# The last half's output: residual stored ahead, scaled tiles accumulated by DMA

## The chip, the cores and the metric

The kernel runs on one core of one Trainium2 chip. The metric is the device time of one execution in microseconds (us), and lower is better. Three runs of the kernel before took 1710.51, 1711.32 and 1711.40 us; the median is 1711.32. Beside them stands one profiled execution, from which all rows below are read.

## The reference

One inference step of a two-layer trunk over 576 tokens (512 of a prompt, 64 of a sample), D_MODEL = 1024, all in float32. Each layer ends like this:

```python
x = x + rmsnorm(merged @ w_o, g_post_mix)
f = jnp.square(jax.nn.relu(rmsnorm(x, g_pre_ffn) @ w1)) @ w2
x = x + rmsnorm(f, g_post_ffn)          # of the last layer, this x is the output
```

`rmsnorm(f, g)` is `f * rsqrt(mean(f * f) + EPS) * g`, the mean over the 1024 features of a token. The change touches only the last line of the last layer: for half of the tokens, the residual `x`, the normed `f` and their sum in the output tensor.

## The kernel before

**Layout.** Everything lies transposed: features on the 128 partitions in KC = 8 tiles, tokens along the free dimension in two halves of NH = 288 (`cols(0)`, `cols(1)`). `x`, `my` (here the output f of the feed-forward network) and the output `x_out` are thus 128 x 8 x 576. A row of one half of one tile is 288 floats, 1152 B.

**Engines.** TensorE does every product as three matmuls of split operands (lines 820 to 822). VectorE and ScalarE make the splits, the activations and the norms. SP's queue loads the weights in order of their use and stores the first half of the output. GpSimd's queue builds sums of weight blocks in DRAM: plain copies (lines 1128, 1129) and accumulating DMAs (`accum_op=ALU.add`, lines 1133, 1137, 1140), done by 1085 us of the span; behind that it does nothing until the tail.

**The last layer's end.** The second matrix w2 gives 16 output tiles, eight of the first half and then eight of the second (`w2_two`); VectorE adds each onto `my` (L3076). The first half's norm and residual (L2162, L2165) are made while the second half is still multiplied, and SP stores that half whole (L1107). For the second half ScalarE writes each tile of `my`, times its gain, into `last` (L2027) and squares it (L1234). When the last square is there, TensorE sums over the features (L4035), ScalarE takes the root (L2037), VectorE inverts it (L3444) and TensorE spreads the factor per token over all partitions into PSUM (L4048). The residual `x[:, :, cols(1)]` is final since the output projection of this layer and is only read from there on.

**The tail** then does, for the eight tiles of the second half, in groups given by two lists (L275), `TAIL_MOVED` = (0, 1), (1, 3), (3, 4) and `TAIL_ADDED` = (4, 6), (6, 8):

- VectorE multiplies `last` by the factor, group by group in that order (L3450), raising `tail_factored` each time;
- for the moved groups GpSimd adds `last` onto `x` (L1196) and raises `tail_moved`, upon which SP stores the group (L1110);
- for the added groups VectorE itself adds (L3453) behind its five products and raises `tail_added`, upon which ScalarE's queue stores the group (L2041).

SP's last instruction waits for all stores (`x_stored`, L1111). Nothing but these semaphores and the order of each engine's instructions, written out by hand, sets the order.

Of the kernel before, what the change touches and what calls it, by code (L numbers as in the profile page):

```python
# [9 lines left out]
ALU = mybir.AluOpType  # L10
# [7 lines left out]
DEPTH = 2  # L18
# [12 lines left out]
KC = D // P  # L31
# [22 lines left out]
def n_head(h, i):  # L54
    return N_P1 + N_HEAD * h + i
# [216 lines left out]

TAIL_MOVED, TAIL_ADDED = [(0, 1), (1, 3), (3, 4)], [(4, 6), (6, 8)]  # L275
TRI = NH // 3

G_PRE, G_POST, G_FF, G_FPOST, G_Q, G_KV, G_CONV = 0, 8, 16, 24, 32, 35, 37
# [69 lines left out]
def root(L, name):  # L348
    return len(ROOTS) * L + ROOTS.index(name) + 1
# [9 lines left out]
def x_new(L, name, m):  # L359
    return 32 * L + NEW[name] + m + 1  # L360
# [6 lines left out]
class Plan:  # L367


    def __init__(self, nc, ctx):  # L370
# [8 lines left out]
        def semaphore(name):  # L379
            return ctx.enter_context(nc.semaphore(name))  # L380
# [111 lines left out]
        self.tail_full = semaphore("tail_full")  # L492
        self.tail_factored = semaphore("tail_factored")
        self.tail_added = semaphore("tail_added")
        self.tail_moved = semaphore("tail_moved")

        self.ff_read = semaphore("ff_read")
        self.ff_inverted = semaphore("ff_inverted")
# [309 lines left out]
def cols(s):  # L808
    return slice(NH * s, NH * (s + 1))
# [40 lines left out]
def program(nc, x_in, consts, tables, blocks, small, uv, cache_t, cache_n, cache_pe,  # L850
            x_out, kv_out, kpe_out, conv_out):
    with ExitStack() as ctx:
        pl = Plan(nc, ctx)
        block = ctx.enter_context(nc.Block())
        loads(nc, block, pl, x_in, consts, tables, blocks, small, uv, cache_t, cache_n, cache_pe, x_out)
        rotation_and_sums(nc, block, pl, blocks)
        scalar_engine(nc, block, pl, x_in, x_out, kv_out, kpe_out, conv_out)
        vector_engine(nc, block, pl)
        tensor_engine(nc, block, pl)


def loads(nc, block, pl, x_in, consts, tables, blocks, small, uv, cache_t, cache_n, cache_pe, x_out):
# [3 lines left out]
    def _(sp):  # L866
# [39 lines left out]
        for L in range(DEPTH):  # L906
# [135 lines left out]
            def w2_load(g, j):  # L1042
                slot_load(L, n_w2(g, j), slot_w2(g, j))
# [59 lines left out]
            w2_load(7, 2)  # L1103
            w2_load(7, 3)

        sp.wait_ge(pl.x_new, x_new(DEPTH - 1, "post_a", KC - 1))
        sp.dma_start(x_out[:, :, cols(0)], pl.x[:, :, cols(0)]).then_inc(pl.x_stored, 16)  # L1107
        for i, (m0, m1) in enumerate(TAIL_MOVED):
            sp.wait_ge(pl.tail_moved, i + 1)
            sp.dma_start(x_out[:, m0:m1, cols(1)], pl.x[:, m0:m1, cols(1)]).then_inc(pl.x_stored, 16)  # L1110
        sp.wait_ge(pl.x_stored, 16 * (1 + len(TAIL_MOVED) + len(TAIL_ADDED)))  # L1111


def rotation_and_sums(nc, block, pl, blocks):


    @block.gpsimd
    def _(pool):

        def first_and_second(n):  # L1120

            L, i = divmod(n, 2 * MIXED)
            row = n_head(FIRST_MIXED + i // 2, (2, 0)[i % 2])
            return blocks[L * NB + row], blocks[L * NB + row + 1]

        def sums_copy(n):
            a, b = first_and_second(n)
            pool.dma_start(pl.sums[n][:, 0:2, :].rearrange("p a k -> p (a k)"), a).then_inc(pl.sums_copied, 16)
            pool.dma_start(pl.sums[n][:, 2:4, :].rearrange("p a k -> p (a k)"), b).then_inc(pl.sums_copied, 16)

        def sums_add_first(n):
            _, b = first_and_second(n)
            pool.dma_start(pl.sums[n][:, 0:4:2, :], b.rearrange("p (a k) -> p a k", a=2), accum_op=ALU.add) \
                .then_inc(pl.sums_first, 16)

        def sums_add_second(n):
            pool.dma_start(pl.sums[n][:, 3, :], pl.sums[n][:, 0, :], accum_op=ALU.add).then_inc(pl.sums_second, 16)

        def sums_add_third(n):
            pool.dma_start(pl.sums[n][:, 1, :], pl.sums[n][:, 3, :], accum_op=ALU.add).then_inc(pl.sums_third, 16)  # L1140

        def sums_steps(n0, n1, first, end):

            for n in range(n0, n1):
                if n < end:
                    pool.wait_ge(pl.sums_copied, 32 * (n + 1))
                if first < n <= end:
                    pool.wait_ge(pl.sums_first, 16 * n)
                if first + 1 < n <= end + 1:
                    pool.wait_ge(pl.sums_second, 16 * (n - 1))  # L1150
                if n > first + 2:
                    pool.wait_ge(pl.sums_third, 16 * (n - 2))
                if n + 1 < end:
                    sums_copy(n + 1)
                if n < end:
                    sums_add_first(n)
                if first < n <= end:
                    sums_add_second(n - 1)
                if n > first + 1:
                    sums_add_third(n - 2)  # L1160

        pool.sem_inc(pl.ring_free, 4)
        pool.sem_inc(pl.w2_free, 4)
        pool.sem_inc(pl.summed, 2)
        pool.sem_inc(pl.pv_read, 1)

        def key_rope(L, half):

            cs, n = cols(half), 2 * L + half
            pool.wait_ge(pl.key_swapped, n + 1)  # L1170
            if half == 1:
                pool.wait_ge(pl.key_roped, n)
            nc.gpsimd.tensor_tensor(pl.rope1_t[:, :], pl.kpe[:, cs], pl.cos[:, cs], ALU.mult) \
                .then_inc(pl.key_turned, 1)
            nc.gpsimd.tensor_tensor(pl.rope1_s[:, half, :], pl.rope1_s[:, half, :], pl.sin[:, cs], ALU.mult) \
                .then_inc(pl.key_turned, 1)
            pool.wait_ge(pl.key_turned, 3 * n + 2)
            nc.gpsimd.tensor_tensor(pl.rope1_t[:, :], pl.rope1_t[:, :], pl.rope1_s[:, half, :], ALU.add) \
                .then_inc(pl.key_turned, 1)
            pool.wait_ge(pl.key_turned, 3 * n + 3)  # L1180
            pool.wait_ge(pl.rooted, root(L, ("rx_a", "rx_b")[half]))
            nc.gpsimd.tensor_tensor(pl.kpe[:, cs], pl.rope1_t[:, :], pl.rx[:, cs], ALU.mult) \
                .then_inc(pl.key_roped, 1)

        pool.wait_ge(pl.x_landed[7], 16)
        sums_copy(0)
        sums_steps(0, BEFORE_KEYS[0], 0, N_SUMS)
        for L in range(DEPTH):
            pool.wait_ge(pl.tables_landed, L * 32 + 32)
            key_rope(L, 0)  # L1190
            key_rope(L, 1)
            last = N_SUMS + 2 if L == DEPTH - 1 else 2 * MIXED * (L + 1) + BEFORE_KEYS[L + 1]
            sums_steps(2 * MIXED * L + BEFORE_KEYS[L], last, 0, N_SUMS)
        for i, (m0, m1) in enumerate(TAIL_MOVED):
            pool.wait_ge(pl.tail_factored, i + 1)
            nc.gpsimd.tensor_tensor(pl.x[:, m0:m1, cols(1)], pl.x[:, m0:m1, cols(1)], pl.last[:, m0:m1, :], ALU.add) \  # L1196
                .then_inc(pl.tail_moved, 1)


def scalar_engine(nc, block, pl, x_in, x_out, kv_out, kpe_out, conv_out):  # L1200
# [924 lines left out]
def vector_engine(nc, block, pl):  # L2125
# [4 lines left out]
    def _(eng):  # L2130
# [1313 lines left out]
        dve.reciprocal(pl.last_root[0:TRI, 0:3], pl.last_root[0:TRI, 0:3]).then_inc(pl.tail_spread, 1)  # L3444
        eng.wait_ge(pl.tail_full, 1)
        eng.wait_ge(pl.tail_scaled, KC)
        for m0, m1 in TAIL_MOVED + TAIL_ADDED:
            factor = pl.att[:, LAST_R:LAST_R + NH].unsqueeze(1).broadcast_to([P, m1 - m0, NH])
            part = pl.last[:, m0:m1, :]
            dve.tensor_tensor(part, part, factor, ALU.mult).then_inc(pl.tail_factored, 1)  # L3450
        for i, (m0, m1) in enumerate(TAIL_ADDED):
            eng.wait_ge(pl.tail_factored, len(TAIL_MOVED) + 1 + i)
            dve.tensor_tensor(pl.x[:, m0:m1, cols(1)], pl.x[:, m0:m1, cols(1)], pl.last[:, m0:m1, :], ALU.add) \  # L3453
                .then_inc(pl.tail_added, 1)

# [706 lines left out]
```

## Time and profile before

| | before |
|---|---|
| median of 3 runs | 1711.32 us |
| profiled execution | 1711.26 us |
| its span | 1709.5 us |
| TensorE busy | 1698.6 us (99% of the span) |
| VectorE, ScalarE, GpSimd busy | 77%, 51%, 6% |
| HBM read, written | 221.20 MB, 60.69 MB |
| DMA issues on SP's, ScalarE's queue for the second half | 3 (144, 288, 144 KB), 2 (288 KB each) |

The span runs from the first to the last event that the profiler recorded; the execution's own time has a little around it. Times below count from the span's start. A matmul's end is modelled, and the busy time of a DMA issue is that of its issuing: when the data has landed stands in a column of its own. The queue of GpSimd is the software queue q0 of the DMA tables, those of SP and ScalarE are the hardware queues q1 and q10.

### The profile page before, as it was taken

How to read it: one execution, taken by the hardware profiler on the slowest of the kernel's cores; microseconds unless marked ns; L12 is line 12 of the kernel's file. 1: busy time of each engine (PE TensorE's matmuls, PEld its weight loads, DVE VectorE, ACT ScalarE, POOL GpSimd, SP SyncE). 2: the span in 40 equal slices, each digit the busy share in tenths (PEclk: the TensorE clock that was granted, in tenths of full speed). 3: DMA queues.
4: the chain of work that ended last, by engine and by line, in shares of the span. 5: the costliest groups of instructions: out<-in, count | busy, mean ns of one | idle time of the engine just before them, and what ended most of it. 6: DMA issues, size and time to landing. Idle time of an engine off the chain costs nothing.

```text
span 1709.5 us, 31894 instructions
## 1 busy us (share of the span) xinstructions
PE 1698.6 (99%) x12687; PEld 1685.4 (99%) x12687; DVE 1324.2 (77%) x2538; ACT 868.9 (51%) x1681; POOL 106.2 (6%) x143
## 2 busy tenths in 40 slices
PE   9999999999999999999999999999999999999997
PEld 9999999999999999999999999999999999999997
DVE  7778877878788777668688788777878887777665
ACT  7636454555554545446366374545545536444452
POOL 1311211000000000000002221000000000000000
PEclk9999999999999999999999999999999999999998
DMA  7889989454321322233138898444623313322231
GB/s 249 219 199 215 252 222 241 125 175 155 112 74 51 112 87 87 87 99 99 62 121 221 209 232 217 133 140 114 201 106 99 99 54 98 97 88 87 74 99 56
DMA packets 94133, 233.64 MB, mean 137 GB/s; under 512 B 9888, under 2 KB 21408, under 8 KB 93984
## 3 DMA queue, kind: packets, MB, share of 16 engines
q1 hardware_dynamic: 72352, 179.16, 32.9%
q0 software_dynamic: 20352, 50.34, 14.6%
q8 instruction: 101, 1.65, 0.4%
q10 hardware_dynamic: 1280, 2.10, 0.3%
q14 instruction: 48, 0.39, 0.1%
HBM read 221.20 MB, written 60.69 MB: 165 GB/s over the span
## 4 chain that ended last, share of the span: by engine, by line
PE 99%; DVE 1%; ACT 0%; issue 0%; DVEq 0%
PE ring L820 20%; PE ring L822 20%; PE ring L821 20%; PE att L820 12%; PE att L822 11%; PE att L821 11%; PE att L3680 1%; PE att L815 1%; PE att L814 1%; PE att L827 0%; PE ring L3516 0%; PE att L3496 0%; PE att L828 0%; PE att L3843 0%; ACT rope_s L1289 0%; PE att L3503 0%
## 5 line engine op out<-in xcount | busy, mean ns | idle before, releaser
L820 PE MATMUL ring<-xs_hi,w_lo 128*128 128x288 f32 x1792 | 532.8, 297 | 0.6 <-issue 0.4
L822 PE MATMUL ring<-xs_hi,w_hi 128*128 128x288 f32 x1792 | 527.9, 295 | 0.0
L821 PE MATMUL ring<-xs_lo,w_hi 128*128 128x288 f32 x1792 | 527.7, 294 | 0.0
L2133 DVE TENSOR_TENSOR w_lo<-w_raw,w_hi 128x1024 fp32r<-128x1024 f32 (+1 forms) x370 | 377.1, 1038 | 27.7 <-ACT w_hi L1218 19.0
L820 PEld LDWEIGHTS ring<-xs_hi,w_lo 128*128 128x128 f32 x1792 | 336.6, 188 | 2.9 <-issue 1.2
L821 PEld LDWEIGHTS ring<-xs_lo,w_hi 128*128 128x128 f32 x1792 | 336.8, 188 | 1.3
L822 PEld LDWEIGHTS ring<-xs_hi,w_hi 128*128 128x128 f32 x1792 | 336.6, 188 | 0.0
L822 PE MATMUL att<-f_hi,w_hi 128*128 128x288 f32 x960 | 283.2, 295 | 0.0
L821 PE MATMUL att<-f_lo,w_hi 128*128 128x288 f32 x960 | 282.9, 295 | 0.0
L820 PE MATMUL att<-f_hi,w_lo 128*128 128x288 f32 x960 | 282.6, 294 | 0.0
L820 PEld LDWEIGHTS att<-f_hi,w_lo 128*128 128x128 f32 x960 | 180.4, 188 | 0.0
L821 PEld LDWEIGHTS att<-f_lo,w_hi 128*128 128x128 f32 x960 | 180.4, 188 | 0.0
L822 PEld LDWEIGHTS att<-f_hi,w_hi 128*128 128x128 f32 x960 | 180.4, 188 | 0.0
L1218 ACT ACTIVATE w_hi<-w_raw 128x1024 fp32r<-128x1024 f32 x124 | 128.7, 1053 | 3.9 <-DMA w_raw<-blocks_in 3.7
L1210 ACT ACTIVATE w_hi<-w_raw 128x1024 fp32r<-128x1024 f32 x98 | 101.8, 1053 | 48.2 <-DMA w_raw<-blocks_in 48.2
L3076 DVE TENSOR_TENSOR my<-att,my 128x288 f32<-128x288 f32 x160 | 69.6, 451 | 61.8 <-PE att L822 61.8
L820 PE MATMUL ring<-turn_hi,w_lo 128*128 128x288 f32 x384 | 114.1, 297 | 0.0
L822 PE MATMUL ring<-mix_hi,w_hi 128*128 128x288 f32 x384 | 113.5, 295 | 0.0
L821 PE MATMUL ring<-turn_lo,w_hi 128*128 128x288 f32 x384 | 113.4, 295 | 0.0
L820 PE MATMUL ring<-mix_hi,w_lo 128*128 128x288 f32 x384 | 113.1, 295 | 0.0
L822 PE MATMUL ring<-turn_hi,w_hi 128*128 128x288 f32 x384 | 113.1, 295 | 0.0
L821 PE MATMUL ring<-mix_lo,w_hi 128*128 128x288 f32 x360 | 105.9, 294 | 0.0
(355 smaller groups left out, 3215.5 us busy)
## 6 DMA issues: line engine op xcount, KB each, us to landing
w_raw<-blocks_in SPq DMA_DIRECT2D x189, 512.0 KB, 3.7
weight_sums<-blocks_in POOLq DMA_DIRECT2D x72, 512.0 KB, 7.0
w_raw<-weight_sums SPq DMA_DIRECT2D x96, 256.0 KB, 4.4
w_raw<-blocks_in SPq DMA_DIRECT2D x70, 256.0 KB, 4.2
weight_sums<-weight_sums POOLq DMA_DIRECT2D x48, 256.0 KB, 6.7
small_raw<-small_in SPq DMA_DIRECT2D x16, 320.0 KB, 5.0
small_raw<-small_in SPq DMA_DIRECT2D x32, 128.0 KB, 5.2
my_kept<-rx SPq DMA_DIRECT2D x12, 288.0 KB, 6.1
```

Of the source, the lines that this page charges most:

```text
L814: pe.matmul(out, both, keys[1], start=False, stop=False)
L815: return pe.matmul(out, both, keys[0], start=False, stop=True)
L820: pe.matmul(out, w[1], x[0], start=first, stop=False)
L821: pe.matmul(out, w[0], x[1], start=False, stop=False)
L822: return pe.matmul(out, w[0], x[0], start=False, stop=last)
L1210: act.activation(hi, raw, ACT.Copy).then_inc(pl.weights_hi, 1)
L1218: act.activation(hi, raw, ACT.Copy).then_inc(pl.weights_hi, 1)
L2133: return dve.tensor_tensor(out, a, hi.bitcast(F32), ALU.subtract)
L3076: dve.tensor_tensor(dst, src, dst, ALU.add).then_inc(pl.w2_free, 1)
L3680: last = pe.transpose(att[:, to:to + P], pl.probs[:, PO[t] + P * j:PO[t] + P * (j + 1)], ident)
```

## The change

The groups are now `TAIL_SUMMED` = (0, 2), (2, 4), (4, 6) and `TAIL_ADDED` = (6, 8). SP stores the residual of tiles 0 to 5 of the second half into `x_out` behind its last weight load. GpSimd no longer adds: it waits for that store, and then for each product issues a DMA that adds the group of `last` (SBUF) onto `x_out` (DRAM). VectorE makes four products and one addition, and ScalarE's queue stores tiles 6 and 7. SP waits for the stores and for the three accumulations.

```diff
-TAIL_MOVED, TAIL_ADDED = [(0, 1), (1, 3), (3, 4)], [(4, 6), (6, 8)]
+TAIL_SUMMED, TAIL_ADDED = [(0, 2), (2, 4), (4, 6)], [(6, 8)]
+SUMMED = TAIL_SUMMED[-1][1]
...
+        sp.wait_ge(pl.x_new, x_new(DEPTH - 1, "wo_b", KC - 1))
+        sp.dma_start(x_out[:, 0:SUMMED, cols(1)], pl.x[:, 0:SUMMED, cols(1)]).then_inc(pl.tail_stored, 16)
         sp.wait_ge(pl.x_new, x_new(DEPTH - 1, "post_a", KC - 1))
         sp.dma_start(x_out[:, :, cols(0)], pl.x[:, :, cols(0)]).then_inc(pl.x_stored, 16)
-        for i, (m0, m1) in enumerate(TAIL_MOVED):
-            sp.wait_ge(pl.tail_moved, i + 1)
-            sp.dma_start(x_out[:, m0:m1, cols(1)], pl.x[:, m0:m1, cols(1)]).then_inc(pl.x_stored, 16)
-        sp.wait_ge(pl.x_stored, 16 * (1 + len(TAIL_MOVED) + len(TAIL_ADDED)))
+        sp.wait_ge(pl.x_stored, 16 * (1 + len(TAIL_ADDED)))
+        sp.wait_ge(pl.tail_summed, 16 * len(TAIL_SUMMED))
...
-        for i, (m0, m1) in enumerate(TAIL_MOVED):
+        pool.wait_ge(pl.tail_stored, 16)
+        for i, (m0, m1) in enumerate(TAIL_SUMMED):
             pool.wait_ge(pl.tail_factored, i + 1)
-            nc.gpsimd.tensor_tensor(pl.x[:, m0:m1, cols(1)], pl.x[:, m0:m1, cols(1)], pl.last[:, m0:m1, :], ALU.add) \
-                .then_inc(pl.tail_moved, 1)
+            pool.dma_start(x_out[:, m0:m1, cols(1)], pl.last[:, m0:m1, :], accum_op=ALU.add).then_inc(pl.tail_summed, 16)
...
-        for m0, m1 in TAIL_MOVED + TAIL_ADDED:
+        for m0, m1 in TAIL_SUMMED + TAIL_ADDED:
...
-            eng.wait_ge(pl.tail_factored, len(TAIL_MOVED) + 1 + i)
+            eng.wait_ge(pl.tail_factored, len(TAIL_SUMMED) + 1 + i)
```

## Rows read from the trace of the kernel before

**Rows 1.** Page: TensorE's busy time, and shares of the chain by engine.
```profile
PE 1698.6 (99%) x12687; PEld 1685.4 (99%) x12687; DVE 1324.2 (77%) x2538; ACT 868.9 (51%) x1681; POOL 106.2 (6%) x143
...
PE 99%; DVE 1%; ACT 0%; issue 0%; DVEq 0%
```

**Rows 2.** Chain of waits, its end: start us, us, what.
```profile
1701.94 2.81 DVE last L3450 x5
1704.76 1.24 DVE x L3453
1706.00 0.67 DVEq L852
```

**Rows 3.** Timeline, tail: start us, us, engine line op out<-in xcount [idle <-releaser].
```profile
1702.48 2.90 POOL L1196 TENSOR_TENSOR x<-x,last 128x288 f32<-128x288 f32 x3 [624.55 <-DVE last L3450]
...
1704.01 0.74 DVE L3450 TENSOR_TENSOR last<-last,att 128x576 f32<-128x576 f32 x1
...
1704.68 1.99 DVE L3453 TENSOR_TENSOR x<-x,last 128x576 f32<-128x576 f32 x2
...
1705.41 0.34 SPq L1110 DMA_DIRECT2D x_out<-x  x1
...
1706.70 0.38 ACTq L2041 DMA_DIRECT2D x_out<-x  x1
```

**Rows 4.** DMA issues at 1690.79, 1705.41, 1706.70: KB each, us to landing.
```profile
x_out<-x SPq DMA_DIRECT2D x1, 1152.0 KB, 5.0
...
x_out<-x SPq DMA_DIRECT2D x1, 144.0 KB, 1.9
...
x_out<-x ACTq DMA_DIRECT2D x1, 288.0 KB, 2.4
```

**Rows 5.** Waits of SP's queue from 1600: us, times, longest.
```profile
SPq L852 <- DMA x_out<-x: 3.3, 1, 3.3
```

**Rows 6.** Last weight loads, their last splits, and the 16 output tiles.
```profile
1647.10 0.80 SPq L868 DMA_DIRECT2D w_raw<-blocks_in  x2
...
1652.79 1.06 ACT L1210 ACTIVATE w_hi<-w_raw 128x1024 fp32r<-128x1024 f32 x1 [0.50 <-DMA w_raw<-blocks_in]
...
1657.04 1.22 DVE L2133 TENSOR_TENSOR w_lo<-w_raw,w_hi 128x1024 fp32r<-128x1024 f32 x1
...
L3076 DVE TENSOR_TENSOR my<-att,my x16: 450/458/458, 1651.0 to 1698.3; 128x288 f32<-128x288 f32 x16
```

**Rows 7.** By line, whole run: ns min/median/max, first and last start.
```profile
L3450 DVE TENSOR_TENSOR last<-last,att x5: 446/744/745, 1701.9 to 1704.0; 128x576 f32<-128x576 f32 x3, 128x288 f32<-128x288 f32 x2
...
L3453 DVE TENSOR_TENSOR x<-x,last x2: 745/1034/1322, 1704.7 to 1705.9; 128x576 f32<-128x576 f32 x2
```

**Rows 8.** GpSimd's accumulating DMA of 256 rows: all 24, then one.
```profile
L1133 POOL DMA_DIRECT2D weight_sums<-blocks_in x24: 886/945/1002, 33.0 to 1051.7; - x24
...
40.86 0.93 POOL L1133 DMA_DIRECT2D weight_sums<-blocks_in  x1
```

**Rows 9.** Landings of GpSimd's DMAs at 33.03 (accumulating), 27.27 (plain), 931.41 (accumulating).
```profile
weight_sums<-blocks_in POOLq DMA_DIRECT2D x1, 512.0 KB, 6.2
...
weight_sums<-blocks_in POOLq DMA_DIRECT2D x1, 512.0 KB, 4.1
...
weight_sums<-weight_sums POOLq DMA_DIRECT2D x1, 256.0 KB, 5.1
```

**Rows 10.** DMA, 35.75 to 38.00: packets, MB, share of 16 engines.
```profile
DMA packets 175, 0.35 MB, mean 156 GB/s; under 512 B 4, under 2 KB 4, under 8 KB 175
...
q0 software_dynamic: 175, 0.35, 93.9%
```

**Rows 11.** DMA, 1692.0 to 1695.4, the store of the first half.
```profile
DMA packets 1040, 1.18 MB, mean 347 GB/s; under 512 B 16, under 2 KB 1040, under 8 KB 1040
```

**Rows 12.** DMA queues, 931.4 to 932.0: packets, MB, share.
```profile
q0 software_dynamic: 43, 0.07, 71.3%
q1 hardware_dynamic: 19, 0.08, 49.2%
```

More of the change, by code:

```diff
@@ L494, in __init__ @@
         self.tail_added = semaphore("tail_added")
-        self.tail_moved = semaphore("tail_moved")
+        self.tail_stored = semaphore("tail_stored")
+        self.tail_summed = semaphore("tail_summed")
         self.ff_read = semaphore("ff_read")
@@ L855, in program @@
         loads(nc, block, pl, x_in, consts, tables, blocks, small, uv, cache_t, cache_n, cache_pe, x_out)
-        rotation_and_sums(nc, block, pl, blocks)
+        rotation_and_sums(nc, block, pl, blocks, x_out)
         scalar_engine(nc, block, pl, x_in, x_out, kv_out, kpe_out, conv_out)
@@ L1104, in _, with rotation_and_sums @@
             w2_load(7, 3)
+        sp.wait_ge(pl.x_new, x_new(DEPTH - 1, "wo_b", KC - 1))
+        sp.dma_start(x_out[:, 0:SUMMED, cols(1)], pl.x[:, 0:SUMMED, cols(1)]).then_inc(pl.tail_stored, 16)
         sp.wait_ge(pl.x_new, x_new(DEPTH - 1, "post_a", KC - 1))
         sp.dma_start(x_out[:, :, cols(0)], pl.x[:, :, cols(0)]).then_inc(pl.x_stored, 16)
-        for i, (m0, m1) in enumerate(TAIL_MOVED):
-            sp.wait_ge(pl.tail_moved, i + 1)
-            sp.dma_start(x_out[:, m0:m1, cols(1)], pl.x[:, m0:m1, cols(1)]).then_inc(pl.x_stored, 16)
-        sp.wait_ge(pl.x_stored, 16 * (1 + len(TAIL_MOVED) + len(TAIL_ADDED)))
-def rotation_and_sums(nc, block, pl, blocks):
+        sp.wait_ge(pl.x_stored, 16 * (1 + len(TAIL_ADDED)))
+        sp.wait_ge(pl.tail_summed, 16 * len(TAIL_SUMMED))
+def rotation_and_sums(nc, block, pl, blocks, x_out):
     @block.gpsimd
```

## The prediction

> **What bounds the kernel now.** I read the page first, from the top: the shares of the engines, then the chain of waits by engine. TensorE is busy for 99% of the span and is 99% of the chain [rows 1]. The change touches no matmul, so it can only act behind the last large one, in the 11.3 us from 1698.2 to the end of the span at 1709.5. There the chain of waits in order of time, the timeline cut into short windows and the DMA issues with their times to landing say what happens. In the chain the reader is to see that everything from 1701.94 on is VectorE and one store: five multiplications (2.81 us), then the two additions, then the queue [rows 2]. The GpSimd additions and the three stores that SP issues for tiles 0 to 3 are not in it: SP's last store is issued at 1705.41 and takes 1.9 us to land, at 1707.3 [rows 3, 4]. What ends last is ACT's store of tiles 6 and 7: issued at 1706.70, landed 2.4 us later, 1709.1 [rows 3, 4]. SP's last wait says the same: 3.3 us from the end of its last issue, 1705.75, is 1709.05 [rows 5]. Behind it 0.4 us pass to the end of the span. The profiled execution took 1711.26 us for a span of 1709.5, so 1.8 us lie around the span; it stands 0.06 us below the median of the runs (1711.32), and I don't correct for that.
>
> **Part 1, the residual of tiles 0 to 5 stored ahead.** One DMA more on SP's queue, 128 x 6 rows of 1152 B, 864 KB. It stands behind the last weight load, which SP issues in the pair at 1647.10 (0.80 us for the two), so it is issued at about 1648. Its own wait (x after the output projection) is long over. The nearest row is the store of the first half, 1152 KB in 5.0 us [rows 4]: at that price it lands by 1653, some 50 us before GpSimd's queue waits for it. It is behind the loads in the same queue, and the last split that waits for those loads idles 0.50 us [rows 6]; TensorE waits for nothing between 1640 and 1698 but its own order (its only waits are the two in the tail). The last split of a weight starts at 1657.0 and takes 1.22 us, so it is done by 1658.3. The weights of the last load are first used by the seventh of the 16 output tiles (order m 0 to 7 of the first half, then of the second), and the 16 come 3.15 us apart (1651.0 to 1698.3) [rows 6]: ten tiles before 1698.2 is 1666.7. The cover is 8.4 us, more than the store's whole 5.0. Cost: 0; without the cover it would be 5.0 us at most. The store of the first half at 1690.79 keeps its place and meets nothing new.
>
> **Part 2, VectorE's work.** Before: multiplications of 1, 2, 1, 2 and 2 tiles, then additions of 2 and 2. After: four multiplications of 2 tiles and one addition. A 576-wide multiplication takes 0.74 us and the next starts 0.67 behind it (1704.01 to 1704.68) [rows 3, 7]. Four start at 1701.94, 1702.61, 1703.28 and 1703.95 and the last ends at 1704.69. The addition now follows its own product at once, so I put 0.05 us between them: it starts at 1704.74. Of the two additions before, one took 1.32 us and one 0.75 [rows 7]; the long one lies beside GpSimd's last addition (it ran to 1705.38) and the short one beside none, and GpSimd adds nothing now. I take 0.75; the other bound is 1.32. It ends at 1705.49, ACT issues the store at 1705.52, and with the 2.4 us of before it lands at 1707.9 (1708.5 at the other bound). **So this branch ends 1.2 us earlier than before**, and that is all the change can give.
>
> **Part 3, the accumulating DMAs.** What goes on GpSimd are three additions (2.90 us in all) and on SP three stores; both were hidden, so nothing is gained. What comes are three DMAs of 288 KB, 256 rows of 1152 B each, out of SBUF and added onto DRAM. The first may start when the first product is done: GpSimd's first addition started 0.09 us behind the product it waits for (1701.94 and 0.45 is 1702.39; it starts at 1702.48) [rows 2, 3, 7], and the product is now twice as wide and ends at 1702.68, so 1702.77. In the issuing itself each takes what the other accumulating DMA of 256 rows takes, 0.95 us median [rows 8]; the third is issued from 1704.67. Nobody else waits in that queue.
>
> No row shows an accumulation out of SBUF, nor rows of 1152 B, so its price is a bound from both sides. The nearest is the accumulation of 512 KB at 33.03, also 256 rows (of 2048 B), with nothing else on the DMA engines: 6.2 us from issue to landing, against 4.1 for a plain copy of the same 512 KB on the same queue [rows 9]. In its steady part (35.75 to 38.00) the 16 engines are 93.9% busy and move 0.35 MB in 2.25 us, 156 GB/s [rows 10], where the plain stores of the first half run at 347 GB/s [rows 11]. So the engines, not GpSimd, set the pace: 0.295 MB at 156 GB/s is 1.9 us a piece, twice the 0.95 us that an issue takes. Three go through as one stream of 0.885 MB. Against the 0.524 MB of the row it has 0.361 MB more, 2.3 us: 6.2 + 2.3 = 8.5 us from the first issue, 1711.3.
>
> One thing crosses that stream: ACT's store of tiles 6 and 7 (0.295 MB at 347 GB/s, 0.85 us of all engines) comes in its midst. Between 0 and 0.85 us; I take the middle, 0.4, since packets of two queues overlap in part (from 931.4 to 932.0 the shares of two queues add up to 120%) [rows 12]. The last accumulation lands at 1711.7.
>
> *Bounds of this part.* Below: paced by the issue alone, the third DMA from 1704.67 at the shortest time to landing that I found for an accumulation, 5.1 us for 256 KB [rows 9]: 1709.8. Below that the accumulation could cost no more than a plain store, rival A. Above: a packet costs the same at 1152 B as at 2048 B. The steady stretch moved 175 packets in 2.25 us, 78 per us; 768 packets instead of 256 are 6.6 us more: 6.2 + 6.6 = 12.8, landing at 1715.6. I stay with the price by bytes, since the plain stores of 1152 B keep 347 GB/s: small rows there cost nothing that shows.
>
> **A rule that speaks for the change.** The row above says 6.2 us for 512 KB. The Trainium skill, "DMA: Bandwidth & Descriptors", section "Anatomy of one DMA — SWDGE (gpsimd) path", gives for a DMA from GpSimd's queue some 2.0 us and its bytes at 436 GB/s. By that a DMA of 288 KB is an estimated 2.7 us and the third would land at 1707.4, hidden under ACT's store. By the row it lands about four us later. The trace sides with the rule for the plain copy (4.1 us against an estimated 3.2) better than for the accumulation (6.2 against the same 3.2).
>
> **Sum.** The accumulation lands at 1711.7 and replaces ACT's store (then 1707.9) as the last to land. Before, the last landing was 1709.1: 2.6 us later. 1711.26 + 2.6 = **1713.9 us**, 0.15% above before. I call a difference under 0.2% (3.4 us) no change, as a measurement of this kernel hardly tells it.
>
> **Rivals.**
> A, *the accumulation is hidden.* It costs what a plain store costs: 2.3 us or so behind an issue at 1704.67 is 1707.0, ACT's store ends last and the gain of part 2 stays whole: 1711.26 - 1.2 = 1710.1 us. For it: sources in SBUF land fast (1.9 to 2.4 us [rows 4]). Against it: I found no accumulation under 5.1 us.
> B, *paced by the issue.* Each DMA's data goes through in the 0.95 us of the next one's issue; last landing 1709.8, 0.7 later than before: 1712.0 us. For it: reading from SBUF leaves only one of the two reads to DRAM. Against it: the 93.9% share.
> C, *a price per packet* (the other side: slower). The place is the 16 engines' queues behind GpSimd's first issue, the price 12.8 us for 768 packets, landing at 1715.6: 1711.26 + 6.5 = 1717.8 us. It decides against the kernel by over 0.2% as soon as the stream and the crossing take 9.7 us instead of my 8.9, thus from a packet price some 15% above that by bytes (0.8 of 5.7 us). For it: an accumulation reads before it writes, and that may be a fixed delay. Against it: 1152-byte rows at full rate in the plain stores.
> D, *GpSimd's queue can't hold three of these DMAs*, and each is written only when the one before has drained. One of 288 KB alone is the row's 6.2 us less 0.229 MB at 156 GB/s (1.5), 4.7; three in a row from 1702.77 end at 1716.9: 1719.1 us. Against it: three DMAs stood in this queue at 40 us (40.34, 40.86 behind 39.81) without a longer issue [rows 8].
> That the change does not do what it says, I see no way for: the stored tiles are final after the output projection, and the queue waits for their landing.
>
> **Chances.** Forecast 0.55, B 0.22, C 0.12, A 0.07, D 0.04. The forecast's own range is 1713.0 to 1715.2 (0 to 0.85 us for the crossing store, half a us for the unmeasured row size). The range of all: 1711.4 leaves A out, 1717.6 leaves out D and the last of C, together under 0.2. Faster by over 0.2%, below 1707.9, is no case at all: 0.01. Slower by over 0.2%, above 1714.7: C, D and the upper quarter of the forecast, 0.30. The rest, 0.69, is no change.
>
> **What would show it.** Four products from 1701.94 to 1704.7 and one addition of 0.75 us behind them; ACT's store issued near 1705.5; GpSimd's three issues near 1702.8, 1703.7 and 1704.7 with some 0.95 us each; software-queue packets until about 1711.5, with a DMA share near full from 1704.5 to the end; SP's last wait on the accumulation. A last wait on ACT's store would be A, a DMA share with gaps between the three would be B or D, packets as long as those of 2048 B would be C. Wrong altogether is the forecast if TensorE's end moves from 1698.2, or if the last landing is before 1710.3 or behind 1713.0.

## The result and the profile after

The changed kernel took 1720.28 us (median of 6 runs, 1719.59 to 1721.55), the kernel before 1710.38 us in the same comparison: ratio 1.0057, 95% interval [1.0046, 1.0068]. That is 9.9 us slower, where 2.6 us slower was forecast and the range ended at 1717.6.

The page of the changed kernel, the lines that answer to [rows 1]:

```profile
span 1719.8 us, 31891 instructions
...
PE 1697.7 (99%) x12687; PEld 1684.5 (98%) x12687; DVE 1324.7 (77%) x2536; ACT 869.2 (51%) x1681; POOL 106.6 (6%) x143
...
PE 97%; DMA 1%; issue 1%; ACT 0%; DVE 0%; SPq 0%; POOL 0%; POOLq 0%; DVEq 0%
```

TensorE is as busy as before; what grew is the stretch behind it. The chain of waits at the end, against [rows 2] (start us, us, what):

```profile
1703.01 1.43 DVE last L3452 x2
1704.44 0.08 issue
1704.52 1.25 POOL x_out L1199
1705.77 3.98 issue
1709.75 1.21 POOL x_out L1199
1710.96 3.74 issue
1714.69 1.24 POOLq L854
```

Before, this was VectorE, VectorE, one store. Now it is GpSimd's queue: three issues, with 3.98 and 3.74 us between them in which GpSimd waits for nothing that the profile shows. Its only semaphore there is `tail_factored`, long raised: the products are over by 1705.76. The timeline of the tail, all engines, against [rows 3]:

```profile
1703.01 2.75 DVE L3452 TENSOR_TENSOR last<-last,att 128x576 f32<-128x576 f32 x4 [1.42 <-PE att L4050]
...
1705.79 0.76 DVE L3455 TENSOR_TENSOR x<-x,last 128x576 f32<-128x576 f32 x1
...
1706.58 0.40 ACTq L2043 DMA_DIRECT2D x_out<-x  x1
...
1704.52 1.25 POOL L1199 DMA_DIRECT2D x_out<-last  x1 [628.63 <-DVE last L3452]
1709.75 1.21 POOL L1199 DMA_DIRECT2D x_out<-last  x1 [3.98 <-issue]
1714.72 1.21 POOL L1199 DMA_DIRECT2D x_out<-last  x1 [3.76 <-issue]
```

What the missing wait is, the landings tell (the three accumulations in turn, then ScalarE's store; KB, us from issue to landing):

```profile
x_out<-last POOLq DMA_DIRECT2D x1, 288.0 KB, 4.9
...
x_out<-last POOLq DMA_DIRECT2D x1, 288.0 KB, 4.6
...
x_out<-last POOLq DMA_DIRECT2D x1, 288.0 KB, 4.6
...
x_out<-x ACTq DMA_DIRECT2D x1, 288.0 KB, 3.6
```

1704.52 + 4.9 is 1709.4, and the second is issued at 1709.75; 1709.75 + 4.6 is 1714.35, and the third is issued at 1714.72. Each starts 0.3 to 0.4 us behind the landing of the one before. The third lands at 1719.3, the span ends at 1719.8.

**Measuring tails.** In the profiled executions the end of TensorE's large matmuls scatters. Most of it arises before 84 us of a run: by the chain of waits the same group of matmuls starts at 83.88 before, at 85.42 in the changed kernel and at 83.12 in e3. I take the start of the last addition onto `my` as the mark of that end: 1698.25 before, 1699.43 after. From it to the end of the span (the tail) are 11.2 us before and 20.4 after: 9.1 us more (unrounded). The other 1.2 us of this profiled execution are scatter; its 1721.55 us is the slowest of the six. Of the 9.9 us between the medians 9.1 are thus placed, and 0.8 are not. The last column counts from the start of VectorE's first product instead. It leaves out the matmuls that spread the factor, which change nothing here and took between 0.91 and 1.45 us. The same measures for all kernels:

| kernel | mark | span | tail | median, ratio to before [95%] | from first product |
|---|---|---|---|---|---|
| before | 1698.25 | 1709.5 | 11.2 | 1710.38 | 7.6 |
| changed | 1699.43 | 1719.8 | 20.4 | 1720.28, 1.0057 [1.0046, 1.0068] | 16.8 |
| e1_ring80 | 1698.85 | 1716.4 | 17.6 | 1719.53, 1.0052 [1.0036, 1.0069] | 14.4 |
| e2_plain | 1698.17 | 1709.0 | 10.8 | 1710.65, 1.0000 [0.9991, 1.0010] | 7.4 |
| e3_rows128 | 1697.24 | 1711.1 | 13.9 | 1713.81, 1.0020 [1.0011, 1.0030] | 10.7 |
| e4_ahead_only | 1698.76 | 1709.5 | 10.7 | 1710.68, 1.0000 [0.9990, 1.0009] | 7.6 |
| e5_six | 1697.94 | 1715.6 | 17.7 | 1717.36, 1.0039 [1.0026, 1.0053] | 14.3 |
| e6_ring68 | 1699.65 | 1718.1 | 18.5 | 1719.86, a single run | 15.3 |
| v1_regroup | 1698.59 | 1709.8 | 11.2 | 1711.31, 1.0006 [0.9997, 1.0015] | 8.0 |
| v2_one_sum | 1698.20 | 1710.5 | 12.3 | 1711.87, 1.0008 [0.9999, 1.0017] | 9.1 |

The kernel before ran at 1710.51 beside e1 to e4 and at 1710.56 beside the rest.

### The profile page after: what moved, and what is told of

It is laid out like the page before. It is cut to its first block, busy times and chain, and to the rows that moved or that the text cites. A ratio compares the mean times of both kernels' runs of the same rounds, so it can differ in the third digit from the quotient of the medians.

```text
span 1719.8 us, 31891 instructions
## 1 busy us (share of the span) xinstructions
PE 1697.7 (99%) x12687; PEld 1684.5 (98%) x12687; DVE 1324.7 (77%) x2536; ACT 869.2 (51%) x1681; POOL 106.6 (6%) x143
## 4 chain that ended last, share of the span: by engine, by line
PE 97%; DMA 1%; issue 1%; ACT 0%; DVE 0%; SPq 0%; POOL 0%; POOLq 0%; DVEq 0%
PE ring L822 20%; PE ring L824 19%; PE ring L823 19%; PE att L822 11%; PE att L824 11%; PE att L823 11%; PE att L3682 1%; DMA w_raw<-blocks_in 1%; PE att L817 1%; PE att L816 1%; PE att L829 0%; PE att L830 0%; PE att L3498 0%; DMA x<-x_in 0%; PE att L3845 0%
```

## The experiments

Two theories for the missing wait. **Ring**: the descriptors of GpSimd's DMAs lie in a scratch that the launch sizes at 1024 bytes (`dynamic_dma_scratch_size`), two accumulations of 256 rows don't fit, and GpSimd waits for room. **Order**: accumulations onto one output, or out of SBUF, take turns whatever the room.

### More scratch

```diff
-    nc = bacc.Bacc("TRN2", ..., dynamic_dma_scratch_size=1024)
+    nc = bacc.Bacc("TRN2", ..., dynamic_dma_scratch_size=1280)
```

> The changed kernel with the scratch for GpSimd's DMA descriptors raised from 1024 to 1280 bytes (the most that the layout leaves room for), nothing else. In the changed kernel GpSimd's three DMAs start 5.2 and 5.0 us apart, each behind the landing of the one before. Theory ring: the queue's room is counted in descriptors, and one accumulating DMA of 256 rows takes more than half of the 1024 bytes, so two don't fit; 1280 bytes hold two but not three. Then the second issue follows the first at once (about 1.25 us apart), the third comes some 5 us after the first, and the end is one round trip, some 4 us, earlier: about 1716 us. Theory order (the accumulations wait for each other whatever the room, because they go onto the same output or out of SBUF): three issues 5 us apart and 1720.3 us as before. Theory room for one byte count: if even 1280 bytes hold only one, also 1720.3.

GpSimd's issues in this run:

```profile
1703.35 2.48 POOL L1199 DMA_DIRECT2D x_out<-last  x2 [634.00 <-DVE last L3452]
1711.10 1.20 POOL L1199 DMA_DIRECT2D x_out<-last  x1 [5.27 <-issue]
```

The first two now stand together, with nothing changed but 256 bytes. That is theory ring, and theory order is out. The time was mis-sized: 1719.53, not 1716. The third issue does not come behind the first landing (1708.2) but behind the second. The two DMAs share the engines and ScalarE's store crosses them (it took 5.3 us to land), so the second lands at about 1710.7 and only 2.8 us of tail are saved. That is the profiled execution, the fastest of the four at 1718.21; by the medians only 0.8 us are saved, and e6, with the same order of issues, saves 1.9 us of tail.

A smaller step narrows the count:

```diff
-    nc = bacc.Bacc("TRN2", ..., dynamic_dma_scratch_size=1024)
+    nc = bacc.Bacc("TRN2", ..., dynamic_dma_scratch_size=1088)
```

> The changed kernel with a scratch of 1088 bytes instead of 1024 (1280 held two accumulations of 256 rows, 1024 one). If the room is counted in units of 16 bytes per DMA engine and an accumulation takes two for each of its 16 rows there and one more at its end, 33, then two take 66, which 1088 bytes (68 units) hold and 1024 (64) don't: the second issue follows the first at once, as with 1280. If the count is another one, the second waits for the landing of the first and the end is where the changed kernel's is.

```profile
1704.27 2.46 POOL L1199 DMA_DIRECT2D x_out<-last  x2 [633.92 <-DVE last L3452]
1712.71 1.21 POOL L1199 DMA_DIRECT2D x_out<-last  x1 [5.99 <-issue]
```

1088 bytes hold two, 1024 hold one. So an accumulation of 256 rows takes more than 512 and at most 544 bytes of the scratch, if each takes the same. The count of 33 units of 16 bytes, 528, lies between. The Trainium skill, "DMA: Bandwidth & Descriptors", section "Terms", gives a descriptor 16 bytes; what these runs show is the bracket, 512 to 544. That an accumulating row takes two units for its two reads fits it and is not shown by itself.

The kernel before already had this wait, at the very place that the prediction read: the next DMA behind the three of 40 us, and the whole run's waits of that line and of the next:

```profile
48.10 0.84 POOL L1137 DMA_DIRECT2D weight_sums<-weight_sums  x1 [6.30 <-issue]
...
POOL weight_sums L1137 <- issue: 130.7, 22, 7.6
...
POOL weight_sums L1140 <- issue: 67.6, 22, 7.3
```

In the program all waits of a step stand ahead of its copies, so nothing in it holds L1137 or L1140. The same lines are L1139 and L1142 in the changed kernels. With 1280 bytes the 22 waits of the first are gone, and with 1088 bytes those of the second; what is left is, in e1 and in e6:

```profile
POOL weight_sums L1142 <- issue: 105.3, 21, 6.8
```

```profile
POOL weight_sums L1139 <- issue: 127.0, 22, 8.0
```

So the scratch bounded GpSimd's queue there too, where GpSimd has no share of the chain of waits [rows 1]. How such a wait ends differs from e1. Of the DMAs in flight at 48.10, the second plain copy had landed (40.34 + 7.5 is 47.8), the accumulation had not (40.86 + 10.8 is 51.7):

```profile
weight_sums<-blocks_in POOLq DMA_DIRECT2D x1, 512.0 KB, 7.5
...
weight_sums<-blocks_in POOLq DMA_DIRECT2D x1, 512.0 KB, 10.8
```

### The same DMAs as plain copies

```diff
-pool.dma_start(x_out[:, m0:m1, cols(1)], pl.last[:, m0:m1, :], accum_op=ALU.add)
+pool.dma_start(x_out[:, m0:m1, cols(1)], pl.last[:, m0:m1, :])
```

> The changed kernel with GpSimd's three DMAs as plain copies instead of accumulations: same rows, same queue, same source and target; left out is that the residual is added for tiles 0 to 5 of the second half. Theory ring (an accumulating row needs two descriptors for its two reads, a plain one only one, so three plain DMAs fit): three issues within 3 us, last landing near 1709.5 and about 1711 us. Theory order (DMAs from this queue onto the same output wait for each other): issues some 4.5 us apart and 1717 to 1719 us. If only accumulations out of SBUF wait for each other, this run looks like theory ring, and the run with more scratch tells them apart.

GpSimd's three issues, and the landings in the tail:

```profile
1703.11 2.26 POOL L1199 DMA_DIRECT2D x_out<-last  x3 [619.89 <-DVE last L3452]
```

```profile
x_out<-last POOLq DMA_DIRECT2D x3, 288.0 KB, 3.0
x_out<-x ACTq DMA_DIRECT2D x1, 288.0 KB, 3.4
```

Three plain DMAs of the same rows fit at once, 0.75 us each. It also measures rival A, the accumulation at the price of a plain store: the time is that of before (ratio 1.0000), not 1.2 us less. ScalarE's store starts 3.57 us behind the first product's start (1701.60 to 1705.17) where it started 4.76 behind it before, so the 1.2 us of VectorE's work are really gone. But it takes 3.4 us to land and not 2.4, beside GpSimd's copies, and most of the gain is given back there.

### Half as many rows, the same bytes

```diff
-("x", (P, KC, NT))
+("x", (P, 2, KC, NH))
...
-pool.dma_start(x_out[:, m0:m1, cols(1)], pl.last[:, m0:m1, :], accum_op=ALU.add)
+pool.dma_start(x_out[:, 1, m0:m1, :].rearrange("p m n -> p (m n)"),
+               pl.last[:, m0:m1, :].rearrange("p m n -> p (m n)"), accum_op=ALU.add)
```

> The changed kernel with the output laid out half by half, 128 x 2 x 8 x 288, so that a group of two tiles is one run of 2304 B in source and target: each accumulation has 128 rows instead of 256, with the same bytes. The scratch stays at 1024 bytes. Theory ring: three accumulations of 128 rows take what one and a half of the old ones took, and all three fit: issues about 1 us apart, the 16 DMA engines as the limit, last landing at 1711 to 1712 and about 1713.5 us, the time that the prediction worked out for its stream. Theory order: issues 4.5 to 5 us apart, 1719 to 1720 us. It also tests the stream's price: 0.885 MB at 156 GB/s.

The issues (the first alone, then the other two), the landings of the first and the third, and the end of the chain:

```profile
1701.84 0.91 POOL L1199 DMA_DIRECT2D x_out<-last  x1 [625.38 <-DVE last L3453]
1702.44 2.09 POOL L1199 DMA_DIRECT2D x_out<-last  x2
```

```profile
x_out<-last POOLq DMA_DIRECT2D x1, 288.0 KB, 4.6
...
x_out<-last POOLq DMA_DIRECT2D x1, 288.0 KB, 7.5
x_out<-x ACTq DMA_DIRECT2D x1, 288.0 KB, 6.7
```

```profile
1701.84 1.80 POOL x_out L1199 x2
1703.65 0.88 POOLq L854
```

At 1024 bytes of scratch three accumulations now stand in the queue, and the tail loses 6.5 us of 20.4. Not all of that is the waiting, since longer rows also cost less per byte; by the 1.8 us worked out under the stream's price below, the waiting is an estimated 4.7 us. The DMA engines set the end: the issues are over by 1704.5, the third accumulation lands at 1710.5 (issued at 1702.98), and ScalarE's store, issued at 1703.97, at 1710.7. 1713.81 us is close to the prediction's 1713.9, in part by luck: that was counted from 1711.26 and had 2.6 us of growth, where the time grew by 3.3 us against its own before, and the stretch from the first product by 3.1.

### Six small accumulations

```diff
-            pool.dma_start(x_out[:, m0:m1, cols(1)], pl.last[:, m0:m1, :], accum_op=ALU.add)...
+            for m in range(m0, m1):
+                pool.dma_start(x_out[:, m, cols(1)], pl.last[:, m, :], accum_op=ALU.add)...
```

> The changed kernel with each accumulation of two tiles issued as two of one tile: six DMAs of 128 rows, 144 KB each, scratch 1024 bytes. By the ring theory the room is for three of 128 rows and not four (the run with 2304-byte rows held three at once). Two forms of it are still open, since with 1280 bytes the third DMA started only when both before it had landed. Form room: a DMA starts as soon as enough of the oldest have drained; then the fourth starts some 0.7 us behind the first landing, and the end is near 1713 us. Form drain: when there is no room, GpSimd waits until all that are in flight have landed; then three, a gap until the third has landed, and three more, with the end near 1716 us. If accumulations out of SBUF simply take turns, six round trips of 4 to 5 us and over 1728 us.

```profile
1702.79 2.68 POOL L1200 DMA_DIRECT2D x_out<-last  x3 [627.48 <-DVE last L3453]
1709.20 2.64 POOL L1200 DMA_DIRECT2D x_out<-last  x3 [3.74 <-issue]
```

Three, a gap, three. The room is for three of 128 rows, and where it is short GpSimd does not go on as the oldest drains: the first lands at 1706.2 (1702.79 + 3.4), the third at 1708.9 (1703.92 + 5.0), and the fourth is issued at 1709.20. That is form drain, as the third DMA of e1 had shown. It is not a rule for this queue: at 48.10 of the kernel before, the issue came while an accumulation was still in flight. One difference is that all accumulations of the tail raise one semaphore, `tail_summed`, while the plain copies and the accumulations of the weight sums raise different ones; no run tests whether that decides it. The end was forecast near 1716 for this form and is 1717.36.

### The early store alone

```diff
+        sp.wait_ge(pl.x_new, x_new(DEPTH - 1, "wo_b", KC - 1))
+        sp.dma_start(x_out[:, 0:6, cols(1)], pl.x[:, 0:6, cols(1)]).then_inc(pl.tail_stored, 16)
```

> The kernel before with the early store of tiles 0 to 5 alone (stored again by the old tail, which waits for it). All theories: the early store costs nothing, 1710.4 us within 1 us, and TensorE's last large matmul ends where it did, within 0.3 us of the paired run's, apart from what the first 110 us of the run shift. If the early store took its 5 us from the last weight loads, 1711 to 1715.

1710.68 against 1710.51, ratio 1.0000 [0.9990, 1.0009]. The early store costs nothing that this interval (some 1.6 us either way) tells. In the changed kernel it took 7.0 us to land behind the weight loads, not 5.0, within the cover of 8.4, and TensorE waited for nothing before the tail.

### Two attempts to use it

The old tail in other groups (GpSimd adds 0, 1 and 2, 3 and 4; VectorE 5 to 7):

```diff
-TAIL_MOVED, TAIL_ADDED = [(0, 1), (1, 3), (3, 4)], [(4, 6), (6, 8)]
+TAIL_MOVED, TAIL_ADDED = [(0, 1), (1, 3), (3, 5)], [(5, 8)]
```

> The kernel before with other groups only: GpSimd adds tiles 0; 1 and 2; 3 and 4, VectorE adds 5 to 7 in one go; no accumulating DMA and no early store. VectorE's additions shrink from 2.0 us to some 1.1, ScalarE's last store starts at about 1706.0 instead of 1706.7 but carries 432 KB; GpSimd ends at about 1706.1 and SP's last store lands near 1708.3. Expected 0.2 to 0.7 us less than before: about 1710 us, at the edge of what can be told.

and one accumulation only, with GpSimd's additions behind it:

```diff
-TAIL_SUMMED, TAIL_ADDED = [(0, 2), (2, 4), (4, 6)], [(6, 8)]
+TAIL_SUMMED, TAIL_MOVED, TAIL_ADDED = [(0, 2)], [(2, 4), (4, 5)], [(5, 8)]
```

> The best use of the accumulation that the findings point to: one DMA only (tiles 0 and 1, so nothing waits for room), early in GpSimd's queue; GpSimd then adds tiles 2 and 3, and 4, VectorE adds 5 to 7. From the product's end to the landing one accumulation took 5.3 us in the changed kernel: 1702.7 + 5.3 = 1708.0 is before the old end. GpSimd is busy with the issue until 1704.7 and ends its additions at 1706.9, SP's last store lands at 1708.8. Expected: the same as before within 0.5 us, 1710.5, thus no gain from accumulating even where the ring is no limit. If the accumulation's packets hold up the stores (3.6 us instead of 2.4 in the changed kernel), up to 1 us slower.

Neither beats the kernel before: 1.0006 [0.9997, 1.0015] and 1.0008 [0.9999, 1.0017], where the first was expected up to 0.7 us faster. Both miss by the same term, VectorE's addition of three tiles, which I had at some 1.1 us (the line in each run; ns min/median/max):

```profile
L3453 DVE TENSOR_TENSOR x<-x,last x1: 2182/2182/2182, 1704.5 to 1704.5; 128x864 f32<-128x864 f32 x1
```

```profile
L3463 DVE TENSOR_TENSOR x<-x,last x1: 3081/3081/3081, 1704.1 to 1704.1; 128x864 f32<-128x864 f32 x1
```

In both, GpSimd is adding when it starts:

```profile
1702.28 3.51 POOL L1196 TENSOR_TENSOR x<-x,last 128x288 f32<-128x288 f32 x3 [628.21 <-DVE last L3450]
```

```profile
1703.66 2.63 POOL L1206 TENSOR_TENSOR x<-x,last 128x576 f32<-128x576 f32 x2
```

GpSimd ends at 1705.79 and 1706.29, and VectorE 0.9 us behind each, at 1706.71 and 1707.22. That looks as if most of the addition ran only when GpSimd's last one was over. No run has this addition of three tiles without GpSimd beside it, so this is argued, not shown; the 1.1 us is an estimate from 0.75 us for two tiles.

## Why the prediction was wrong

**The step that failed** is "Three go through as one stream", together with the reason that left rival D at 0.04: "three DMAs stood in this queue at 40 us ... without a longer issue". The row was right and the reading was not: I counted DMAs where the ring counts descriptors, and I looked at the issues and not at the wait behind them. Those three were two plain copies of 128 rows and one accumulation of 256, and the next DMA of the queue stood 6.30 us idle before 48.10, with no releaser. The new ones are three accumulations of 256 rows, and no row of before had two such DMAs in flight. What the runs showed in its place is rival D: one accumulation in the queue at a time, two waits of 3.98 and 3.74 us, and a last landing 16.3 us behind the first product's start where the prediction had 9.8. Rival D put the time at 1719.1. The 1024 bytes stood in the launch, in the code that I had read.

**The size of D.** Its round of 4.7 us was 5.2 and 5.0 measured. From the first product's start (1703.01) to the first landing (1709.4) are 6.4 us, then two rounds make 1719.3, 16.3 us in all. Before, the last landing was 7.2 us behind that start (1701.94 to 1709.1). 16.3 - 7.2 = 9.1, the whole growth of the tail. The release of GpSimd was mis-sized too: its DMA starts 0.6 to 0.75 us behind the end of the product, not 0.09, and each issue takes 1.21 to 1.25 us, not 0.95. [rows 3] had the 0.09 of an addition, which is no measure for a DMA.

**Part 1** held: 0 us, as closely as e4 can tell.

**Part 2** held as far as the issue of ScalarE's store, 1.2 us earlier (3.57 us behind the first product in place of 4.76). Its landing did not: 3.6 us in the changed kernel, 3.4 beside plain copies and 6.7 beside three accumulations, against 2.4. The prediction let the store slow the accumulations (0.4 us) and forgot that they slow it.

**The stream's price** held where it could run, with rows of 2304 B: in e3 the last accumulation landed 8.7 us behind the first issue (1701.84 to 1710.5), forecast 8.9. For rows of 1152 B it would have been too low. One accumulation of the changed kernel alone on the engines (DMA, 1711.4 to 1714.2):

```profile
DMA packets 272, 0.29 MB, mean 105 GB/s; under 512 B 16, under 2 KB 272, under 8 KB 272
...
q0 software_dynamic: 272, 0.29, 89.2%
```

0.892 x 16 engines x 2.8 us over 272 packets is 147 ns a packet. The row of before was 193 ns with 2048 B (0.939 x 16 x 2.25 over 175) [rows 10]; by bytes 1152 B would be 109, by packets 193. That row reads its source from DRAM, but e3 gives the same picture out of SBUF: 201 ns with 2304 B (1.115 x 16 x 1.6 over 142, from 1704.6 to 1706.2). So the truth lies about halfway between the forecast's price and rival C's. With a ring for three, the changed kernel's stream would have been an estimated 1.8 us longer than forecast (768 x 38 ns over 16 engines); that was not tried.

**The rule** that was weighed, 2.0 us and the bytes at 436 GB/s from the Trainium skill, "DMA: Bandwidth & Descriptors", section "Anatomy of one DMA — SWDGE (gpsimd) path", gives an estimated 2.7 us for 288 KB. The traces come near it for plain DMAs of this queue, 3.0 us in e2, and disagree for accumulations, 4.6 to 4.9 in the changed kernel, as the row of before had said.

**What would have shown it** was named: gaps in the DMA share between the three. That is what the profile shows: no packet moved from 1709.9 to 1711.3 or from 1714.5 to 1716.2.

## What to carry to other kernels

Before moving work onto a software DMA queue, count what its descriptor ring holds in rows and not in DMAs: here an accumulation of 256 rows took more than half of 1024 bytes, the next one waited for its landing, and a layout with half as many rows took 6.5 us off the time. Idle time of GpSimd between DMAs with no releaser is the sign to look for; the kernel before had it 22 times at each of two lines. An observed burst of DMAs is evidence only for bursts of that kind and row count. And work that is taken off the critical engine gains no more than the last landing does: with plain copies in place of the accumulations, 1.2 us of VectorE's work were gone and the time did not change measurably.

## What the runs showed of the hardware

- GpSimd's ring: 1024 bytes hold three accumulations of 128 rows but not four, and one of 256 but not two; 1088 and 1280 hold two. When there is no room the next issue waits, and the profile shows this as idle time with no releaser. In the tail it waited until all in flight had landed (e1, e5, e6); at 48.10 of the kernel before it came 0.3 us behind the plain copies' landing, with an accumulation still in flight.
- A DMA on that queue starts 0.6 to 0.75 us behind the end of the product that releases it, where a GpSimd addition starts 0.1 behind it.
- An accumulating packet costs 147 ns at 1152 B and 201 ns at 2304 B out of SBUF, and 193 ns at 2048 B out of DRAM.
- A store of 288 KB from ScalarE's queue takes 2.4 us beside no DMA of GpSimd's, 3.4 beside its plain copies and 6.7 beside three accumulations.
- VectorE's addition with both inputs in SBUF takes longer while GpSimd adds: 2.18 and 3.08 us (v1, v2) where an estimated 1.1 us was due. Before, this had shown as 1.32 against 0.75 [rows 7].
